# The first inverse factor of the backward direction is made by VectorE instead of GpSimd, behind each half of N

## The reference

```python
def chunk_gated_delta(q, k, v, g, beta):
    ...
    decay = jnp.exp(jnp.where(incl, diff, -jnp.inf))
    kb = k * beta[..., None]
    a_low = jnp.where(strict, jnp.einsum("bhnid,bhnjd->bhnij", kb, k) * decay, 0.0)
    lower = a_low + jnp.eye(c, dtype=a_low.dtype)
    rhs = jnp.concatenate([v * beta[..., None], kb * jnp.exp(gc)[..., None]], axis=-1)
    sol = lax.linalg.triangular_solve(lower, rhs, left_side=True, lower=True,
                                      unit_diagonal=True)
    ...
def deltanet_mixer(xn, w_in, conv_w, a_log, dt_bias, out_g):
    ...
    o_f = chunk_gated_delta(q, k, v, g[..., :h_], beta[..., :h_])
    o_b = flip(chunk_gated_delta(flip(q), flip(k), flip(v),
                                 flip(g[..., h_:]), flip(beta[..., h_:])))
```

## Time and profile before

| | |
|---|---|
| median of 3 runs | 2359.72 us (2359.61 to 2362.69) |
| the profiled execution | 2358.7 us, its span 2356.9 us |
| granted TensorE clock | 0.999 of full |
| TensorE matmul busy | 2337.8 us, 99% |
| VectorE busy | 1546.3 us, 66% |
| ScalarE busy | 1250.4 us, 53% |
| GpSimd busy | 156.5 us, 7% |

### The profile page before, as it was taken

The page is one execution under the profiler, slowest core; times in us unless marked ns, Lnnn a source line. Parts: engine busy times, 40 slices in busy tenths (PEclk is TensorE's granted clock), DMA queues, the critical chain, the costliest instruction groups (busy, mean ns, idle before and its releaser), DMA issues.

```text
span 2356.9 us, 36109 instructions
## 1 busy us (share of the span) xinstructions
PE 2337.8 (99%) x11967; PEld 1981.4 (84%) x11967; DVE 1546.3 (66%) x2471; ACT 1250.4 (53%) x2322; POOL 156.5 (7%) x114
## 2 busy tenths in 40 slices
PE   9999999999999999999999999999999999999998
PEld 7888888878888888888888888888888888888887
DVE  6668778688677665557665565556677555676555
ACT  6656566465455554445554455555555444455444
POOL 0012021120001000001000000000111000011000
PEclk9999999999999999999999999999999999999999
DMA  9664364353356666666666576566666666666665
GB/s 334 172 177 134 99 174 121 111 177 101 121 176 190 189 192 194 193 187 185 186 189 194 193 208 172 161 184 196 189 189 189 194 193 191 186 185 186 193 193 176
DMA packets 232553, 423.00 MB, mean 179 GB/s; under 512 B 27885, under 2 KB 29806, under 8 KB 232302
## 3 DMA queue, kind: packets, MB, share of 16 engines
q1 hardware_dynamic: 231709, 420.28, 59.5%
q10 hardware_dynamic: 720, 1.06, 0.1%
HBM read 419.14 MB, written 2.10 MB: 179 GB/s over the span
## 4 chain that ended last, share of the span: by engine, by line
PE 96%; DVE 2%; ACT 1%; issue 0%; DMA 0%; POOLq 0%; POOL 0%; ACTq 0%; DVEq 0%
PE pair L517 19%; PE pair L519 19%; PE pair L518 19%; PE pair L536 10%; PE aux L536 10%; PE aux L538 5%; PE pair L538 5%; PE aux L715 4%; PE aux L565 2%; DVE w_lo L1528 1%; DVE r L1756 1%; PE aux L754 0%; PE aux L691 0%; PE aux L743 0%; PE aux L974 0%
## 5 line engine op out<-in xcount | busy, mean ns | idle before, releaser
L1528 DVE TENSOR_TENSOR w_lo<-raw,w_hi 128x512 fp32r<-128x512 f32 x1536 | 1088.6, 734 | 614.1 <-ACT w_hi L1016 611.0
L1016 ACT ACTIVATE w_hi<-raw 128x512 fp32r<-128x512 f32 x1536 | 939.6, 633 | 773.2 <-DMA raw<-in_ffn_w 624.1
L517 PE MATMUL pair<-w_hi,hid_hi 128*128 128x512 f32 x1012 | 394.3, 390 | 0.0
L519 PE MATMUL pair<-w_hi,hid_lo 128*128 128x512 f32 x1012 | 393.8, 389 | 0.0
L518 PE MATMUL pair<-w_lo,hid_hi 128*128 128x512 f32 x1012 | 393.7, 389 | 0.0
L517 PE MATMUL pair<-w_hi,xT 128*128 128x512 f32 x960 | 386.4, 403 | 1.4 <-DVE xT L1600 0.7
L519 PE MATMUL pair<-w_hi,xT 128*128 128x512 f32 x960 | 375.5, 391 | 0.0
L518 PE MATMUL pair<-w_lo,xT 128*128 128x512 f32 x960 | 374.8, 390 | 0.0
L536 PE MATMUL pair<-xT,w_hi 128*128 128x512 f32 x1024 | 360.9, 396 | 0.4 <-DVE h L2033 0.2
L536 PE MATMUL aux<-xT,w_hi 128*128 128x512 f32 x1024 | 359.1, 395 | 0.0
L538 PE MATMUL aux<-xT,w_lo 128*128 128x256 f32 x1024 | 287.2, 280 | 0.0
(11 more groups left out here) (247 smaller groups left out, 1604.0 us busy)
## 6 DMA issues: line engine op xcount, KB each, us to landing
raw<-in_ffn_w SPq DMA_DIRECT2D x1024, 256.0 KB, 3.0
raw<-in_dn_w_in SPq DMA_DIRECT2D x208, 256.0 KB, 2.9
raw<-in_tok_w_out SPq DMA_DIRECT2D x128, 256.0 KB, 3.0
raw<-in_gm_w_in SPq DMA_DIRECT2D x112, 256.0 KB, 2.9
raw<-in_mem_w_kv SPq DMA_DIRECT2D x64, 256.0 KB, 3.2
r<-in_mem_columns SPq DMA_DIRECT2D x8, 256.0 KB, 4.9
h<-in_x_columns SPq DMA_DIRECT2D x8, 256.0 KB, 5.1
h<-in_mem_columns SPq DMA_DIRECT2D x8, 256.0 KB, 3.4
```

The costliest lines, as they stand in the source:

```text
L517: pe.matmul(acc, act_hi[:, kt, tokens], w_hi[:, slot], start=start, stop=False)
L519: mm = pe.matmul(acc, act_lo[:, kt, tokens], w_hi[:, slot], start=False, stop=last and k == 1)
L1016: act.activation(w_hi[:, slot], raw[:, slot], ACT.Copy).then_inc(hi_ready, 1)
L1528: dve.tensor_tensor(w_lo[:, slot], raw[:, slot], w_hi[:, slot].bitcast(F32), ALU.subtract).then_inc(tiles_split, 1)
```

## The change

The two GpSimd instructions for each half go, and VectorE does the same two, at the end of the stage that makes that half of `NT`. The semaphore is renamed; ScalarE and TensorE wait for the same counts of it as before.

```diff
@@ tensor, level 0
-                                pe.wait_ge(sem("x0_pool"), g * 4 + 4)
+                                pe.wait_ge(sem("x0_back"), g * 4 + 4)
@@ scalar
-                    act.wait_ge(sem("x0_pool"), g * 4 + (2 * m + 1))
+                    act.wait_ge(sem("x0_back"), g * 4 + (2 * m + 1))
                     free(act.activation(NT[:, 1, m].rearrange("p h i -> p (h i)"), bank(n)[:], ACT.Copy), n)
...
@@ vector, the stage of each half of N
                         free(e, n)
+                    have(DG + 2 * m)
+                    have(DG + 2 * m + 1)
+                    dst = XL[:, 1, m]
+                    dve.tensor_tensor(dst, NT[:, 1, m], over(cst[:, C_M1L:C_M1L + P], 4), ALU.mult).then_inc(sem("x0_back"), 1)
+                    dve.wait_ge(sem("x0_back"), g * 4 + (2 * m + 1))
+                    dve.tensor_tensor(dst, dst, over(ident, 4), ALU.add).then_inc(sem("x0_back"), 1)
                     if m == 1:
                         attention_part()
                     yield
@@ gpsimd
-                for m in range(2):
-                    have(DG + 2 * m)
-                    have(DG + 2 * m + 1)
-                    dst = XL[:, 1, m]
-                    pool.tensor_tensor(dst, NT[:, 1, m], over(cst[:, C_M1L:C_M1L + P]), ALU.mult).then_inc(sem("x0_pool"), 1)
-                    pool.wait_ge(sem("x0_pool"), g * 4 + (2 * m + 1))
-                    pool.tensor_tensor(dst, dst, over(ident), ALU.add).then_inc(sem("x0_pool"), 1)
```

More of the change, by code:

```diff
@@ L1287, in deltanet @@
                         else:
-                            act.wait_ge(sem("x0_pool"), g * 4 + 4)
+                            act.wait_ge(sem("x0_back"), g * 4 + 4)
                         act.activation(Xodd[:, d].rearrange("p x (b s) -> p x b s", s=s),
```

## The result

The change made the kernel slightly slower: 2364.22 us (median of 20, 2361.18 to 2366.77) against 2359.68 (median of 20, 2356.88 to 2363.34). The profiled execution has a span of 2363.6 us against 2356.9, and about half of these 6.7 us have causes that the prediction didn't have.

The account below looks back on a forecast made before the run. TensorE, busy 99% of the span, was taken to bound the kernel, right behind VectorE in three stretches. Losses of 1.75 + 0.65 + 0.54 = 2.94 us gave 2362.7 us against the median, range 2359.3 to 2366.5.

Parts of the forecast that it names:

- TensorE stands right behind VectorE in the three stretches: One stretch in each of groups 0 to 2: VectorE is late there, so whatever it takes on delays TensorE.
- A pair costs 1.44 us: VectorE's two new instructions per half of N take 0.12 + 0.72 + 0.60 us; six pairs 8.6 us.
- group 0: First stretch: two tiles wait for splits delayed by the pairs, so L715 starts 1.75 us later.
- group 1: Second stretch: transposes 0.34 us later, then the next tile waits for its split; L715 starts 0.65 us later.
- The relief is eight holds of 1.10: GpSimd's instructions no longer hold VectorE's splits: 2 + 3 + 3 holds in the groups, 8.8 us in sum.
- It isn't paid when it is due: In the three stretches the balance is nearly zero, but VectorE's pair comes first and the relief behind it.
- Group 2: +0.54: Third stretch: L1738 moves by 1.78 us, an earlier wait for L1852 disappears, leaving 0.54 us lost.
- the clock stays at 1.00: TensorE's granted clock in the stretches: stalls of 1 to 3 us, as before, left it at 1.00.
- rival A: ScalarE's three waits for GpSimd's multiply are on the path after all: 7.4 us faster, 2352.3 us; chance 3%.
- rival B: Slow splits aren't GpSimd's doing, or VectorE's new instructions meet it: no relief, 8.6 us slower, 2368.3 us; chance 8%.
- The sum: Whole kernel: 1.75 + 0.65 + 0.54 = 2.94 us slower over the three groups.

Follow-up runs that it names:

- e4: The change with each VectorE pair placed two splits later, against the kernel before: 2357.83 us, ratio 0.9993 (0.9983 to 1.0003).
- e6: The change with both VectorE pairs behind N and its splits, against the kernel before: 2357.73 us, ratio 0.9994 (0.9985 to 1.0003).
- e5: Backward factor's pair left out on both engines, with all waits for it, against the kernel before: 2353.37 us, ratio 0.9974 (0.9965 to 0.9983).
- e3: The change plus five zero matmuls on TensorE in group 2's wait, against the kernel before: 2362.30 us, ratio 1.0007 (0.9998 to 1.0016).
- e2: VectorE makes the backward factor in group 2 only, GpSimd in groups 0 and 1, against the kernel before: 2361.05 us, ratio 1.0004 (0.9995 to 1.0013).
- e0: The change itself measured again, against the kernel before: 2363.05 us, ratio 1.0015 (1.0006 to 1.0024).
- e1: The change with L1738 ahead of the second pair in group 2, against the kernel before: 2361.63 us, ratio 1.0006 (0.9997 to 1.0015).
- e7: Kernel before with GpSimd's pairs kept and VectorE making extra pairs at the change's places, against before: 2375.19 us, ratio 1.0072 (1.0057 to 1.0086).
- e10: The kernel of e4 measured once more, against the kernel before: 2359.64 us, ratio 1.0003 (0.9993 to 1.0013).
- e8: GpSimd's pairs kept in group 0, VectorE's pairs behind N's splits in groups 1 and 2, against before: 2359.77 us, ratio 0.9999 (0.9987 to 1.0011).
- e9: The kernel of e6 measured once more, against the kernel before: 2357.53 us, ratio 0.9995 (0.9984 to 1.0007).

## Why the prediction was right, step by step

**TensorE stands right behind VectorE in the three stretches.** Right: all new waits of TensorE are for L1528, L1837 and L1738, and moving VectorE's work (e4, e6) or leaving it out (e5) moves TensorE.

**A pair costs 1.44 us.** It costs 1.53. The step took one wait for a fresh result at 0.12; ahead of L1846 stand two, and they cost 0.19, and L1848's another 0.01. Two pairs are 0.18 more, which is the error in group 0 (1.92 for 1.75); in group 1 only 0.06 of it shows (0.71 for 0.65).

**The relief is eight holds of 1.10.** Right: no split over 0.69 in the stretches, VectorE's busy time as before. (Its 0.68 + 3 x 0.60 is 2.48 and not 2.49, which changes nothing.)

**It isn't paid when it is due.** Right, and the core of the case. The same pairs cost +3.3 us by the traces where they stand ahead of the splits and L1738, and -0.7 to -0.8 behind them.

**Group 2: +0.54.** Right as worked out, +0.60 in e3. What failed is the sentence that the clock stays at 1.00 since stalls of 1 to 3 us had left it so. The kernel before has one wait of 2.53 us there and kept its clock. The change added a second wait to the first, 2.94 and 1.55 us with 1.06 of transposes between, and the clock then fell in the three traces that have both (the change and e2 with those lengths, e0 with 1.41 and 1.55), but not in e1, which has the first alone at 1.41, nor in e3, which has 0.74 us of waits left. In e7 it fell in group 2 within a wait of 4.99 us for L1838. That idle time of TensorE makes it fall rests on e3, which changes only what TensorE does in the wait, on one trace and eleven executions. That it takes two waits isn't shown, and e7's falls behind one wait of 2.8 us in groups 0 and 1 speak against it. It adds 1.4 to 2.9 us in the three traces, but not in every execution: of the 20 of the change, the six with a mean clock of 0.999 average 2363.1 us, the six with 0.997 average 2365.1.

**ScalarE's 7.4 us of waits aren't on the path** (rival A). Right, by e6.

**No relief** (rival B). Refuted: the holds are gone from the trace of the change, and e7, the change's work without its relief, is 17.0 us slower than before where the change is 3.8.

**The sum.** 1.95 + 0.75 + 0.60 = 3.3 us by the traces, plus the clock in some executions, and less 1.1 if before has executions with the hold in its group 0. The measured +3.8 and +3.5 lie between; how often each case occurs is open, since every run has one trace. The forecast of +2.9 is the mechanism's 3.3 with the pair sized too small; that the measured time lies so near it, although the clock's part wasn't in the sum, is partly luck.

## What to carry to other kernels

When work moves to an engine that others stand right behind, a balance of its busy time is not enough: ask which instruction that is waited for comes directly behind the new ones, and put them behind it. Here that was the whole difference between +3.3 and -0.8 us. Look at what a helping engine does to the one it helps; here no list of waits named it, only stretched durations did. And where a change lengthens TensorE's idle time, read the granted clock there, since that can cost more than the wait: in group 2 of the change it cost 2.9 us beside 0.6.

## What the runs showed of the hardware

- The granted clock fell behind a wait of TensorE of 2.5 us (at L743 of group 2, the products with `g_up`, waiting for L1569; between 514 and 524 us) in 8 of the 12 traces of the change and e0 to e10, and not in the trace of before. The instructions at that place are the same in all of them, and so is the wait, 2.45 to 2.50 us. The kernel before may have it in other executions: 27 of its 91 have a mean clock of 0.998 instead of 0.999. The stretches at half clock are 3.4 us long there, 6.8 near 540 in the change and 10.2 in e7. Near 520 a fall costs 0.1 us at L715 (the kernel of e4: -0.53 with it, -0.65 without, in e10), since TensorE waits for VectorE a little later anyway.
- Whether a GpSimd instruction or VectorE's next split goes first isn't settled by which starts first in the records: with the same 0.23 us between them it went both ways (before, against e2 and e8).
- The MLP of layer 0, which nothing here changes, had two speeds of TensorE at a granted clock of 1.00. Line L536 between 700 and 840 us (duration min/median/max, ns), before:

```profile
L536 PE MATMUL aux<-xT,w_hi x213: 391/391/391, 699.6 to 839.7; 128*128 128x512 f32 x107
```

And in e4:

```profile
L536 PE MATMUL aux<-xT,w_hi x205: 395/398/404, 699.8 to 839.7; 128*128 128x512 f32 x103
```

In e4 one L536 with the L538 behind it takes 0.353 us instead of 0.346, which makes it about 3 us longer in that stage alone, and e5, e6 and e9 have the same pace there. Other stages do it too: from L715 of group 2 to the end, where nothing was changed, it takes 1814.3 to 1814.8 us in eight traces, 1817.3 to 1817.5 in e4, e5 and e6, and 1811.1 and 1811.2 in e7 and e9. Why is open. It is as large as what this study looks for, and the reason why the distances between named instructions are trusted here above the times.
